# A streaming encoder layer on one core: the order of the first norms in the opening, on ScalarE, VectorE and TensorE

## The reference: what is computed

```
x += 0.5 * post(SwiGLU_1(pre(x)))       # first half-step FFN, 1024 -> 2*2816 -> 1024
h = pre(x); z = h @ W_in                # gated recurrence, pooling, gates
x += post(W_out(sigmoid(gA)*yA + sigmoid(gB)*yB))
x += 0.5 * post(SwiGLU_2(pre(x)))
x += post(sigmoid(pre(x) @ W_pg) * (p @ W_pp))

def rmsnorm(x, g):                      # pre and post
    y = xf * lax.rsqrt(jnp.mean(xf * xf, axis=-1, keepdims=True) + EPS)
    return y * g
```

## Time and profile before

| what | value |
|---|---|
| median of 3 runs | 2325.48 us (2324.36 to 2325.75) |
| the profiled execution, its own time | 2328.06 us |
| span from its first to its last instruction | 2326.3 us |
| PE busy | 2258.1 us, 97% of the span |
| DVE busy | 1516.5 us, 65% |
| POOL busy | 1335.9 us, 57% |
| ACT busy | 1283.8 us, 55% |

### The profile page before, as it was taken

How to read it: one execution, slowest core, us unless ns; L and a number is a source line. 1 busy time by engine, 2 the same in 40 slices (tenths; PEclk the granted TensorE clock), 3 DMA queues, 4 the chain that set the end, 5 groups by cost and what they waited for, 6 DMA issues and landing times.

```text
span 2326.3 us, 54611 instructions
## 1 busy us (share of the span) xinstructions
PE 2258.1 (97%) x20456; PEld 1936.0 (83%) x20456; DVE 1516.5 (65%) x2563; ACT 1283.8 (55%) x2423; POOL 1335.9 (57%) x1019
## 2 busy tenths in 40 slices
PE   8899999999998999999999999999999999999998
PEld 6788888888887888888778888877888888888886
DVE  7877767635589677667872232489687777445755
ACT  6454555533577677777563433665554554335775
POOL 2777777767613665555644443316878778676120
PEclk9999999999999999999999999999999999999999
DMA  3123222343430111111111112331232222545202
GB/s 133 51 79 105 78 95 87 125 155 120 162 102 26 41 45 53 41 43 57 43 48 41 54 63 81 109 101 37 78 106 77 87 77 88 185 126 193 70 19 76
DMA packets 155246, 195.09 MB, mean 84 GB/s; under 512 B 13168, under 2 KB 102512, under 8 KB 155120
## 3 DMA queue, kind: packets, MB, share of 16 engines
q1 hardware_dynamic: 111920, 153.59, 20.9%
q10 hardware_dynamic: 43200, 39.83, 5.2%
HBM read 155.49 MB, written 37.88 MB: 83 GB/s over the span
## 4 chain that ended last, share of the span: by engine, by line
PE 72%; DVE 12%; POOL 5%; ACT 5%; issue 4%; DMA 2%; SPq 1%; ACTq 0%; DVEq 0%; POOLq 0%
PE bank L1083 18%; PE bank L1086 18%; PE bank L1085 18%; PE bank L1050 4%; PE bank L1052 4%; PE bank L1051 4%; POOL ring L944 2%; DVE hid L2275 2%; DMA ring<-weights 2%; POOL ring L948 1%; DVE ops L2439 1%; DVE hid L2429 1%; DVE ops L2330 1%; DVE ops L2283 1%; PE bank L1225 1%
## 5 line engine op out<-in xcount | busy, mean ns | idle before, releaser
L1083 PE MATMUL bank<-ops,ring 128*128 128x264 f16 x4112 | 1139.4, 277 | 25.3 <-DVE ops L2439 8.8
L1086 PE MATMUL bank<-ops,ring 128*128 128x264 f16 x4112 | 1138.6, 277 | 0.0
L1085 PE MATMUL bank<-ops,ring 128*128 128x264 f16 x4112 | 1138.6, 277 | 0.0
L944 POOL TENSOR_TENSOR ring<-ring 128x512 f16<-128x512 f32 (+1 forms) x492 | 645.2, 1331 | 292.2 <-ACT ring L1445 292.2
L1445 ACT ACTIVATE ring<-ring 128x512 f16<-128x512 f32 (+1 forms) x492 | 286.7, 615 | 506.8 <-POOL ring L948 503.8
L1083 PEld LDWEIGHTS bank<-ops,ring 128*128 128x128 f16 x4112 | 403.4, 98 | 96.6 <-DVE ops L2439 10.4
L1086 PEld LDWEIGHTS bank<-ops,ring 128*128 128x128 f16 x4112 | 403.6, 98 | 61.7
L1085 PEld LDWEIGHTS bank<-ops,ring 128*128 128x128 f16 x4112 | 403.7, 98 | 60.4
L929 POOL TENSOR_TENSOR ring<-wtmp,ring 128x512 f16<-128x512 f32 x107 | 132.1, 1240 | 344.1 <-ACT ring L1386 343.5
L1050 PE MATMUL bank<-hid,ring 128*128 128x264 f16 x1068 | 294.9, 276 | 2.5 <-issue 1.3
L1052 PE MATMUL bank<-hid,ring 128*128 128x264 f16 x1068 | 294.8, 276 | 0.0
(11 more groups left out here) (234 smaller groups left out, 3540.3 us busy)
## 6 DMA issues: line engine op xcount, KB each, us to landing
ring<-weights SPq DMA_DIRECT2D x363, 256.0 KB, 2.8
ops<-spill SPq DMA_DIRECT2D x16, 1056.0 KB, 6.6
ring<-weights SPq DMA_DIRECT2D x120, 128.0 KB, 2.5
spill<-hid ACTq DMA_DIRECT2D x42, 264.0 KB, 3.0
spill<-hid ACTq DMA_DIRECT2D x20, 528.0 KB, 5.0
ops<-spill SPq DMA_DIRECT2D x8, 792.0 KB, 4.8
hid<-xT SPq DMA_DIRECT2D x8, 528.0 KB, 8.2
hid<-out_x ACTq DMA_DIRECT2D x8, 528.0 KB, 8.9
```

The lines of the kernel that those rows point to most:

```text
L944: nc.gpsimd.tensor_tensor(low(slot, kh), weight_source(name, k, kh), high(slot, kh), ALU.subtract)\
L1083: nc.tensor.matmul(out, whi, xhi, start=(kk == 0 and fresh(name, k)), stop=False, skip_group_check=True)
L1085: nc.tensor.matmul(out, whi, xlo, start=False, stop=False, skip_group_check=True)
L1086: mm = nc.tensor.matmul(out, wlo, xhi, start=False, stop=end, skip_group_check=True)
```

## The change

Three edits, all in the opening. PE does `norm(1)` no longer right behind `norm(0)` but behind chunk 2 of position 1. ACT does `norm(0)` and part 0 of `h_high` ahead of unit 2, then parts 1 and 2, unit 3, part 3, unit 4, and `norm(1)` as before. DVE leaves the second half of quarter 1's squares until the whole of `h_split(0, 0)` is issued.

```
-            norm(1)
-            up(0, {(6, 2): calls(2), (10, 2): calls(3)})
+            up(0, {(1, 2): calls(1), (6, 2): calls(2), (10, 2): calls(3)})
...
-            prep("ffn1_up0", 0, 0, 1, 2)
+            prep("ffn1_up0", 0, 0, 1)
             norm(0)
-            h_high(0, 0, (0, 1))
+            h_high(0, 0, (0,))
+            prep("ffn1_up0", 0, 2)
+            h_high(0, 0, (1, 2))
             prep("ffn1_up0", 0, 3)
-            h_high(0, 0, (2,))
+            h_high(0, 0, (3,))
             prep("ffn1_up0", 0, 4)
-            h_high(0, 0, (3,))
             norm(1)
...
-            for g in range(2):
-                for n, ks in enumerate(parts_of(SQUARE_PARTS)):
-                    x = xk(0, g, ks.start, ks.stop)
-                    dve.wait_ge(x_loaded[g][n], 16)
-                    V_.tensor_tensor(hq(0, g)[:, ks, :], x, x, ALU.mult).then_inc(own_squares, 1)
+            def first_squares(g, n):
+                ks = parts_of(SQUARE_PARTS)[n]
+                x = xk(0, g, ks.start, ks.stop)
+                dve.wait_ge(x_loaded[g][n], 16)
+                V_.tensor_tensor(hq(0, g)[:, ks, :], x, x, ALU.mult).then_inc(own_squares, 1)
+
+            first_squares(0, 0)
+            first_squares(0, 1)
+            first_squares(1, 0)
             h_split(0, 0)
+            first_squares(1, 1)
             h_split(0, 1)
```

## The result

| | before | changed |
|---|---|---|
| median, 15 executions of each | 2325.48 us (2323.11 to 2332.76) | 2335.52 us (2329.94 to 2344.37) |
| profiled execution, its own time | 2328.06 us | 2335.52 us |
| its span | 2326.3 us | 2333.4 us |
| norm(0) ends on PE | 12.87 us | 12.28 us |
| norm(2) starts on PE | 36.18 us | 41.81 us |

The ratio of the two is 1.0033 with a 95% interval of 1.0023 to 1.0044: the changed kernel is slower, as forecast, but 2335.52 lies above the range (2328.3 to 2333.1). Of the 7.1 us between the two spans, 5.6 are there at norm(2) and 1.5 come behind it.

What follows compares the result with a forecast made beforehand. PE, busy 97% of the span, was taken to bound the kernel, so only its gaps could be won. 0.35 + 3.56 + 0.5 + 0.7 = 5.1 us on the 2325.48 us median gave 2330.6 us, range 2328.3 to 2333.1.

Steps and rivals of the forecast that it cites:

- Norm(0) ahead of unit 2: In the opening, ACT's Ln can start 0.04 us behind the sum, at 12.91 instead of 12.99: 0.08 us won.
- The parts of quarter 0: In the opening, low parts come later behind ACT and POOL; PE starts part 3 at 21.33, before 20.98: +0.35 us.
- norm(1) in the stream: Sixteen passes of 0.2225 us at 2.4 GHz, now among PE's position 1 matmuls: +3.56 us.
- Unit 5: Behind the moved norm(1), PE waits for ACT's and POOL's work on this unit: +0.5 us.
- The clock: PE's 3.3 us idle behind norm(0) halves its rate until 22 us, slowing part 2: +0.7 us, bounds 0 to 2.4.
- the clock comes back late, at 25.4: In the opening, position 1 and half of norm(1) run at half rate: +1.7 us, so 2332.3; chance 0.18.
- The shift reaches the end: Behind norm(2) no idle absorbs a shift, so all 5.1 us reaches the kernel's end.
- From one profile to a median: Whole kernel: the median of 2325.48 us plus the opening's 5.1 us gives 2330.6 us.

Runs made afterwards that it cites:

- the doubled one: The changed kernel with norm(1)'s eight matmuls done twice at their new place in PE's stream: 2334.55 us (1.0031).
- the late units: The kernel before, with ACT's units 3 and 4 put behind all four parts of quarter 0: 2327.59 us (1.0001), and 2324.63 us (0.9995) when run again.
- fillers: Four fp32 matmuls into a free bank at each of two PE waits in the heads: on the late units 2329.85 us, on the changed kernel 2334.41 us.
- two repeats: The changed kernel run again, unchanged, in two later sets: 2330.97 us (1.0017) and 2332.99 us (1.0021).
- the changed kernel's third: The changed kernel run a third time, unchanged: 2332.99 us (1.0021 against the kernel before).
- the half: The changed kernel with the first four chunks of norm(1) left right behind norm(0), only the last four at the new place: 2331.05 us (1.0022).
- the warmed kernel: The changed kernel with seven extra fp32 matmuls right behind norm(0), keeping PE at work where it was idle: 2330.47 us (1.0014).

## Why the prediction was right in direction and too low

Point by point, by its own steps:

- *Norm(0) ahead of unit 2:* in the changed profile the Ln starts 0.10 us behind norm(0)'s end (12.38 and 12.28), where 0.04 was said. PE sets the time, as argued, and the freed ACT waited 2.04 us for it. Right.
- *The parts of quarter 0:* +0.35 predicted, +0.41 measured with ACT's edit alone. Low part 1 did end 0.57 behind POOL. Right. (By the rule of the Trainium skill, SBUF — State Buffer, "Who interferes with whom", that the blocked one waits until the other ends, it would have ended its whole 0.70 behind; the trace differs from it by 0.13, before by 0.14. The moved square, 1.26 us when alone, ended 1.12 behind POOL, again 0.14 short of its length, so the difference looks like a constant of the record and not like work done beside POOL; that is argued, since the profile's ends on POOL are rough.) The moved square was priced at 1.3 to 1.8 us and took 2.21, at no cost to PE.
- *norm(1) in the stream:* +3.56 predicted and measured (24.23 to 27.79), and the doubled one grew by as much and 0.1 to 0.6 more, which is its clock's.
- *Unit 5:* a wait on POOL's line 929 of 0.35 us, 0.5 us in all by taking it away; norm(1)'s end to norm(2) 14.02 us, said 14.0. Right.
- *The clock:* **this step failed in size.** "With the gaps between the parts I take 22" put the rise at 22 us and priced it at 0.7; it came at 23.7, 24.5 and 25.7 us, and the price was 1.7 to 2.3. The rival "the clock comes back late, at 25.4", at +1.7 more and a chance of 0.18, is what the opening did, within its price. The row that I leaned on the earlier trace rows had PE busy without gaps behind its idle; here PE worked 1.35 us in each 2.25, and the half-rate matmuls of parts 1 and 2 did not bring the clock back. What was wrong was taking a rise seen under steady work as the measure for work with gaps. The one kernel in which PE came back from the same idle to work almost without gaps, PE's edit alone, had its clock back after 5.4 us, close to the 5.2 of the earlier trace rows; the changed kernel needed 8.1 to 9.2 (9.2 in the one whose clock, like that of PE's edit alone, had fallen before PE's return). That is one profile against three, and no run varied the gaps alone. Nor is the earlier trace rows a sure sign that the clock falls: in the profile of the changed kernel the same wait of 2.80 us ended at 76.06, and the clock stayed at 1.00:

```profile
76.06 0.29 PE L1083 MATMUL bank<-ops,ring 128*128 128x264 f16 x1 [2.80 <-DVE hid L2413]
```

```profile
76.06:79.40 3.34, 3.34 (x30) 2.92 (x31) 3.24 (x5) 1.15 (x2) 2.48 (x3) 1.00 0.23 78
```

- *The shift reaches the end:* yes. In the three profiles of the changed kernel norm(2) to the end is 2291.6, 2286.6 and 2284.5 us, against 2290.1, within the scatter that the kernels without the edit show too (2283.5 to 2292.8 for the late units). The wait on line 2439 grew instead of absorbing.
- *From one profile to a median:* **this step failed too.** The sum took the opening's 5.1 us as the difference of two medians, and the range added up the opening's terms alone, with nothing for how far medians of this kernel move from set to set. The three sets came out at +10.0, +4.4 and +7.2 us.

The opening so loses 29.53 to 30.08 less 23.31, 6.2 to 6.8 us by the distance from norm(0), and 5.6 to 7.0 by the plain start of norm(2). Over the three sets of runs the changed kernel's median is 2332.2 us (37 executions) and that of the kernel before, on the same chips, 2326.2 (71 executions): 5.9 us, which is about the opening's loss and would lie inside the predicted range. So the correction of the clock's term, 1.0 to 1.6 us, explains 2331.6 to 2332.2, and 3.3 to 3.9 us of the predicted set's median stay over.

What these are, the traces tell in part. In the predicted set's profiled execution 1.5 us lie behind norm(2). They are not the heads, which took 832.6 us here and 832.5 before, but the second FFN: from about 1568 us to the sum of squares near 2155 it is 1.7 us longer, and PE waited once more on line 1113 for DVE's line 2310 (9.4 us in eight waits between 500 and 2200 us, before 8.0 in seven). This profile of before was itself one with the long heads, 2.6 us above its median.

Behind norm(2) the profiles without fillers differ by how long the granted clock was 0.50 on the way to the last norm: with 20.5 us of it 2290.1 to 2291.6 us, with 10.2 us 2283.5 to 2284.5, with 13.6 and 17.1 us 2285.0 to 2287.3, and 2292.8 once. The changed kernel's three have 20.5, 17.1 and 10.2 us, the one of before 20.5, the three others with PE's old order 10.2 to 17.1. So no traced execution shows that the change adds half rate behind norm(2).

The record also holds the mean granted clock, to 0.001, of every execution but those of before in the predicted set. In the predicted set six executions had 0.994 and took 2331.0 us on average, and nine had 0.991 to 0.993 and took 2337.9. The two repeats have 12 executions at 0.994 or 0.995, of 2329.9 us on average, and 10 at 0.991 to 0.993, of 2334.7. So the excess of the predicted set is in its low-clock executions, 9 of 15, with means higher than in the repeats. The mean clock of all 37 is 0.9930, that of the 114 of before in the other sets 0.9946. The difference of 0.0016 is what the opening's own 6.8 to 10.2 us at half rate make (0.0015 to 0.0022), so on average nothing points to more half rate elsewhere. Why one set of 15 had more slow executions than the two others is not shown; that stays open.

## What to carry to other kernels

Work of PE that seems free because PE would otherwise idle can be doing two jobs: taken away, it costs its own length where it lands, and the idle time that it leaves behind can halve PE's rate through the work that follows. Price such a step from a stretch in which PE returned to work *with the same gaps*: here the rise seen under steady work came 5.2 to 5.4 us after PE's start, and the one with gaps 8.1 to 9.2 us after it. An edit that costs 0.4 us by itself can cost more beside another that lowers the clock, so measure the two together as well. And where the scatter of the times is as large as the effect, compare distances between two fixed instructions in the trace before comparing medians, start from an instruction that nothing else holds up, and leave room in the forecast for the scatter of the medians.

## What the runs showed of the hardware that was not expected

- In this opening the half rate lasted 6.8 us in five profiles and 10.2 us in three (the doubled norm, the changed kernel's third, the changed kernel with fillers), though the changed kernel and the doubled one run the same program up to there.
- It came without a long idle: behind waits of 1.58 and 1.39 us in the half, and not behind 0.34, 1.39 and 1.40 in the warmed kernel. The same wait was followed by it in some executions and not in others: the one of 2.1 us in the heads, and the one of 2.80 us near 70 to 77 us, which was in the profile of before and not in the changed kernel's first two.
- In the heads, half rate over 3.4 us near 1145 us cost more than the slow matmuls: 1.7 us in them and 1.9 in a later wait on ACT's line 2037, 3.6 in all.
- Where DVE's low part met POOL at work it ended 0.57 us behind POOL (17.25 and 17.82) in the changed kernel, and 0.56 in the one before.
